# Two tiles begun on the un-normalised input behind three layer norms, and index items placed beside attention turns, in a two-block network on one core

## The chip, the cores and the metric

The kernel runs on one core of a Trainium2 chip. The metric is the device time in microseconds; the lower the better. The engines are TensorE (PE, matmuls; PEld its weight loads), VectorE (DVE), ScalarE (ACT), GpSimd (POOL) and SyncE (SP, which issues the weight transfers).

## The reference

Two blocks run one after the other on x of 512 positions by 1024 features, all in float32. The first block (RWKV, sparse attention, memory attention) isn't touched. The second has two layers; each is mixer, layer norm, SwiGLU, layer norm. The first mixer is a top-k attention, the second an HGRN2 recurrence:

```python
rel = relu(einsum('bqhd,bsd->bhqs', qib, k_idx))        # 8 index heads
score = einsum('bqh,bhqs->bqs', wb, rel)                # then the causal mask
_, sel = lax.top_k(score, topk)                         # softmax attention over sel
...
h = layer_norm(DEEPNORM_ALPHA * h + mix, ln_g[layer, 0], ln_b[layer, 0])
ffn = (silu(h @ w_gate[layer]) * (h @ w_up[layer])) @ w_down[layer]
h = layer_norm(DEEPNORM_ALPHA * h + ffn, ln_g[layer, 1], ln_b[layer, 1])
```

A layer norm is (x - mean)/sqrt(var + eps) * g + b over the 1024 features. So for a weight matrix W the product with a normalised position is r * (W'(g x)) + s * (W'g) + W'b, with r the inverse root and s = -mean * r of that position.

## The kernel before

x lies transposed, as 8 tiles (k) of 128 features by 512 positions. All dense weights come as a stream of 229 slabs of 128 by 1024 (one output tile of 128 features, 8 k). SP loads them into a ring of four (`load_slabs`, line 101); a slab's place in the ring is free when it is split. Each slab and each input is cut in a high part, which ACT casts to the fast matmul type (`cast_slab`, line 145), and a low part, which DVE takes as the difference (`split_slab`, line 150). `product` (lines 176 to 178) does a tile with three matmuls: high by high, high by low, low by high. A slab against the whole input is 24 matmuls of 128 by 512. Two slabs hold parts at a time (three in HGRN); `place_third` gives one slab further room.

The program is a list of stages. Between two stages all engines meet at a barrier. Within one, each engine runs its own hand-written list, tied by semaphores. The stages here are: `stage_dsa` (attention), `stage_project` "wo", `stage_ffn` 0, `stage_hgrn`, `stage_project` "ho", `stage_ffn` 1, `stage_store`.

A layer norm is cut over two stages. `Norm` ends the first. Per output tile DVE adds the residual (lines 1935, 2137) and sums x (1747), ACT squares (1730), POOL adds squares (1738). PE sums the accumulators and the last tile over the features by ones-columns (1758, 64 instructions in all), DVE and ACT make r and s (1795 to 1806), PE does four warm-up matmuls (184), then spreads r and s over 128 rows (1777). ACT and DVE cast and split the next three slabs. `Apply` opens the second stage: DVE multiplies by r and adds s (1831, 1834), ACT applies g and b twice, for the high part and for x (1845, 1847), POOL takes the low part (1853). PE does ten warm-ups and then `first_pair`, the first two slabs k by k as low parts come; then the other slabs.

In `stage_ffn` slabs alternate between gate and up. ACT takes Silu of the gate bank (2081) and casts the product (2084), DVE multiplies (2115) and takes its low part (2118); eleven turns of two hidden tiles. In `stage_hgrn` each of 8 heads has four slabs: forget gate (sigmoid), value, query (Silu), output gate (Silu), taken by ACT at line 2848 into SBUF; between them it does Ln (2878) and four Exps (2886 to 2896) for the decays. PE's `turned` transposes values and keys (2745, 2751) into banks 2 and 3; inner products begin at line 2765.

In `stage_dsa` 24 index items (3 query blocks of 128 positions by 8 heads; the first block needs none) go first: PE makes the scores against all keys so far (2589; 256, 384 or 512 columns), ACT takes Relu (2604), DVE adds them up with the head's weight (2619, 2622). Then follow 68 turns of `Attend`, one a unit (a head of a query block): PE scores (1204), DVE masks and takes the minimum (1257), ACT takes Exp (1235), three turns later PE transposes (1215) and a turn after sums (1226); a turn n has one `pick` for n up to 47 (2635, 2636), two DVE operations that find and strike the next eight largest scores. Sixteen picks make a block's mask, which the units 16 and more need. `fill` says how many warm-ups PE does ahead of a unit's transposes:

```python
fill = {n: 1 if n > 16 else 2 for n in range(4, len(units)) if begin.group_of(n + Attend.TURN, 0) is None} | {3: 10, 16: 6}
```

Of the kernel before, what the change touches and what calls it, by code (L numbers as in the profile page):

```python
# [6 lines left out]
F32 = mybir.dt.float32  # L7
# [60 lines left out]
class Ctx:  # L68
# [58 lines left out]
    def place_third(self, n, tile):  # L127

        at = self.bigr[:, tile:tile + 4, :].rearrange("p a b -> p (a b)")
        self.third = {n: at.rearrange("p (a k c) -> p a k c", a=2, k=KT)}  # L130
# [9 lines left out]
    def cast_slab(self, act, n, i=0):  # L140

        act.wait_ge(self.slab_ready[n % RING], 16 * (n // RING + 1) + i * 16)
        if n >= self.held and n not in self.third:
            act.wait_ge(self.slab_done, n - self.held + 1 + i * RING)
# [64 lines left out]
def first_pair(c, pe, slab, x):  # L209
# [3 lines left out]
    for k in range(KT):  # L213
        x.wait(pe, k)
        for u in range(2):
            mm = product(pe, c.bank[u][:, :], c.slab_parts(slab + u, k), x.tile(k), k == 0, k == KT - 1)
            if k == KT - 1:
                mm.then_inc(c.slab_done, 1)
# [104 lines left out]
def stage_in(c):  # L323
# [36 lines left out]
    with nc.Block() as block:  # L360
# [106 lines left out]
        def _(pe):  # L467
# [83 lines left out]
            first_pair(c, pe, 0, hp)  # L551
# [1160 lines left out]

class Norm:
# [4 lines left out]
    def __init__(self, c, tag, squares, at, kind, g, b=None, eps=1):  # L1718
        self.squares = squares
# [7 lines left out]

    def scalar_square(self, act, added, m):
        wait_tile(act, added, m)
        act.activation(self.squares[:, m, :], self.c.x[:, m, :], ACT.Square).then_inc(self.sq_out, 1)  # L1730

    def pool(self, pool):

        for m in range(1, KT - 1):
            pool.wait_ge(self.sq_out, m + 1)
            if m > 1:
                pool.wait_ge(self.sq_added, m - 1)
            pool.tensor_tensor(self.acc[:, 1, :], self.squares[:, 0, :] if m == 1 else self.acc[:, 1, :],
                               self.squares[:, m, :], ALU.add).then_inc(self.sq_added, 1)
# [10 lines left out]
    def tensor(self, pe, added):  # L1750

        c = self.c
        one = con(c, "ones")[:, 0:1]

        def sums(bank, x, first):
            for q in range(QT):
                for half in HALVES:
                    mm = pe.matmul(bank[half, q:q + 1], x[:, q * P:(q + 1) * P][:, half], one, start=first and q == 0,
                                   stop=not first, skip_group_check=True)
            return mm  # L1760

        wait_tile(pe, added, KT - 3)
        if self.kind == "ln":
            pe.wait_ge(self.x_added, KT - 2)
            sums(c.bank[0], self.acc[:, 0, :], True)
        pe.wait_ge(self.sq_added, KT - 2)
        sums(c.bank[1], self.acc[:, 1, :], True)
# [1493 lines left out]
```

## Time and profile before

| | us |
|---|---|
| median of three runs | 1902.44 (1901.03 to 1903.01) |
| the profiled execution | 1900.69 |
| its span | 1898.8 |
| PE busy | 1811.3 (95%) |
| DVE busy | 897.9 (47%) |
| ACT busy | 781.5 (41%) |
| POOL busy | 246.2 (13%) |

The span is what the trace covers; 1.9 us of the execution lie around it. Matmuls are pipelined: their rows overlap, and the distance between starts is the cost of one. The granted clock of PE is given as a share of 2.4 GHz, so 0.50 is the lower level, 1.2 GHz. Rows of a timeline give start, duration, engine, line, operation, result and operands, shape, count, and in brackets the idle time before it with what ended it. All times of rows count from the span's start.

### The profile page before, as it was taken

The page shows a single profiled execution, that of the slowest core. Times are in us where ns is not written, and L with a number is a line of the kernel's source. Part 1 is how long each engine was busy: PE and PEld are TensorE (multiplying, and loading weights), DVE is VectorE, ACT ScalarE, POOL GpSimd, SP SyncE. Part 2 cuts the span into 40 slices and gives each one's busy share as a digit, 9 for nine tenths or more (in the row PEclk, how much of TensorE's full clock was granted, in tenths as well). Part 3 has the DMA queues.
Part 4 walks back from the last instruction along what each step waited for, and adds up shares of the span by engine and source line. Part 5 has one row for each costly group of instructions (what it writes and reads, how often), then busy time and mean ns, then how long its engine had stood idle before and what let it go on. Part 6 is the DMA issues. An engine that isn't in the chain of part 4 may idle for free. (4 is left out here: it accounts for less than half of the span.)

```text
span 1898.8 us, 31549 instructions
## 1 busy us (share of the span) xinstructions
PE 1811.3 (95%) x12642; PEld 1419.9 (75%) x12642; DVE 897.9 (47%) x1644; ACT 781.5 (41%) x1341; POOL 246.2 (13%) x205
## 2 busy tenths in 40 slices
PE   6999999899899899999999999999998999999996
PEld 5776666576775666778888888788887778888885
DVE  2673554555557796343333323654554533333223
ACT  4543444455443445342323222765563333222222
POOL 3011232000125000120000000322320210000000
PEclk9999999899999899999999999999999999999998
DMA  5231101200121000213323233222221222332331
GB/s 185 89 92 66 35 25 36 84 23 12 45 74 45 1 1 1 75 64 95 99 99 91 97 100 98 66 87 69 77 67 31 92 75 91 99 99 94 95 100 45
DMA packets 38488, 134.00 MB, mean 71 GB/s; under 512 B 4896, under 2 KB 5344, under 8 KB 38112
## 3 DMA queue, kind: packets, MB, share of 16 engines
q1 hardware_dynamic: 37504, 130.07, 21.5%
q8 instruction: 87, 1.43, 0.3%
q10 hardware_dynamic: 864, 2.23, 0.3%
q14 instruction: 33, 0.27, 0.0%
HBM read 129.40 MB, written 2.10 MB: 69 GB/s over the span
## 5 line engine op out<-in xcount | busy, mean ns | idle before, releaser
L150 DVE TENSOR_TENSOR big_parts<-ring,big_parts 128x1024 fp32r<-128x1024 f32 x181 | 226.7, 1256 | 532.6 <-ACT big_parts L145 531.2
L176 PE MATMUL bank<-h_parts,big_parts 128*128 128x512 f32 (+1 forms) x1072 | 423.9, 395 | 8.3 <-DVE big_parts L150 4.9
L177 PE MATMUL bank<-y_parts,big_parts 128*128 128x512 f32 (+1 forms) x1072 | 417.2, 389 | 0.0
L178 PE MATMUL bank<-h_parts,big_parts 128*128 128x512 f32 (+1 forms) x1072 | 417.2, 389 | 0.0
L145 ACT ACTIVATE big_parts<-ring 128x1024 fp32r<-128x1024 f32 x181 | 191.3, 1060 | 382.9 <-PE bank L178 380.1
L176 PEld LDWEIGHTS bank<-h_parts,big_parts 128*128 128x128 f32 x1072 | 201.9, 188 | 59.0 <-POOL y_parts L1853 6.8
L178 PEld LDWEIGHTS bank<-h_parts,big_parts 128*128 128x128 f32 x1072 | 201.8, 188 | 42.0
L177 PEld LDWEIGHTS bank<-y_parts,big_parts 128*128 128x128 f32 x1072 | 202.0, 188 | 39.4
L176 PE MATMUL bank<-big_parts 128*128 128x512 f32 x352 | 136.9, 389 | 0.0
L177 PE MATMUL bank<-work_parts,big_parts 128*128 128x512 f32 x352 | 136.9, 389 | 0.0
L178 PE MATMUL bank<-big_parts 128*128 128x512 f32 x352 | 136.9, 389 | 0.0
L1235 ACT ACTIVATE work<-work 128x256 f32<-128x256 f32 (+4 forms) x128 | 67.1, 524 | 110.9 <-DVE work L1257 110.5
L184 PE MATMUL bank<-cst 128*128 128x256 f32 x356 | 101.1, 413 | 8.2 <-PEq L92 8.2
L176 PE MATMUL bank<-h_parts,work_parts 128*128 128x512 f32 x232 | 93.9, 405 | 1.2 <-PEq L92 0.8
L184 PEld LDWEIGHTS bank<-cst 128*128 128x128 f32 x356 | 70.8, 207 | 28.1 <-issue 15.5
L1257 DVE CUSTOM_DVE_ANT_0 work<-bank,big 128x256 f32<-128x256 f32 (+4 forms) x128 | 56.8, 444 | 73.2 <-PE bank L1204 63.7
L178 PE MATMUL bank<-h_parts,work_parts 128*128 128x512 f32 x232 | 90.5, 390 | 0.0
L177 PE MATMUL bank<-y_parts,work_parts 128*128 128x512 f32 x232 | 90.4, 390 | 0.0
L832 PE MATMUL bank<-x,ring 128*128 128x512 f32 x176 | 85.7, 610 | 0.2 <-ACT big L1031 0.2
L150 DVE TENSOR_TENSOR work_parts<-ring,work_parts 128x1024 fp32r<-128x1024 f32 x37 | 46.2, 1252 | 76.9 <-ACT work_parts L145 76.8
L177 PEld LDWEIGHTS bank<-work_parts,big_parts 128*128 128x128 f32 x352 | 66.1, 188 | 13.8
L176 PEld LDWEIGHTS bank<-big_parts 128*128 128x128 f32 x352 | 66.1, 188 | 13.7
(399 smaller groups left out, 2696.1 us busy)
## 6 DMA issues: line engine op xcount, KB each, us to landing
ring<-in_wstream SPq DMA_DIRECT2D x229, 512.0 KB, 3.6
x<-in_xt SPq DMA_DIRECT2D x8, 512.0 KB, 6.7
out_t<-x SPq DMA_DIRECT2D x8, 256.0 KB, 2.0
work<-in_memt ACTq DMA_DIRECT2D x1, 1024.0 KB, 14.2
y<-in_cw SPq DMA_DIRECT2D x1, 1024.0 KB, 5.0
cst<-in_cst ACTq DMA_DIRECT2D x1, 768.0 KB, 7.9
cos<-in_reset SPq DMA_DIRECT2D x2, 256.0 KB, 6.8
big<-work SPq DMA_DIRECT2D x4, 128.0 KB, 4.5
```

Of the source, the lines that this page charges most:

```text
L145: act.activation(self.place(n)[:, 0, :, :], self.ring[:, n % RING, :, :], ACT.Copy).then_inc(self.slab_cast, 1)
L150: dve.tensor_tensor(self.place(n)[:, 1, :, :], self.ring[:, n % RING, :, :], self.place(n)[:, 0, :, :].bitcast(F32), ALU.subtract).then_in ...
L176: pe.matmul(out, w[0], x[0], start=start, stop=False, skip_group_check=True)
L177: pe.matmul(out, w[0], x[1], start=False, stop=False, skip_group_check=True)
L178: return pe.matmul(out, w[1], x[0], start=False, stop=stop, skip_group_check=True)
L184: pe.matmul(bank[:, 0:2 * P], con(c, "ident"), c.cst[:, 0:2, :], start=True, stop=True)
L832: mm = pe.matmul(c.bank[DENSE_BANK][:, :], c.raw_slab(n, k), c.x[:, k, :], start=k == 0, stop=k == KT - 1)
L1235: act.activation(e, e, ACT.Exp, bias=self.low[:, n:n + 1], scale=-1.0, accum_out=self.den[:, n:n + 1])\
L1257: dve.tensor_tensor_reduce(self.weights(n), self.c.bank[self.SCORES[n % 3]][:, 0:u.keys], u.mask, -self.scale, 3e38, ALU.add, ALU.min, sel ...
```

## The change

Behind the norms of "wo", `stage_ffn` 0 and "ho" the first two slabs of the next stage are multiplied with g x, not with the normalised input. `Raw` makes the parts of g x per tile (ACT casts with g as scale, DVE takes the low part) in the stage before, and PE multiplies the raw slabs in the ring with the columns g and b (`columns`). The ones-column sums of the accumulators go ahead of the stage's last product (`early`), k = 0 and 1 of the two slabs stand where the warm-ups were, k = 2 to 7 open the next stage; there the second two slabs run k by k with the normalised input into banks 2 and 3. ACT copies the two finished banks, DVE applies r and s to them (`open_tile`), and W'b comes as a bias. Four slabs are cast and split by the stage's end, not three. In the feed-forward the fifth slab waits for the first product tile. In HGRN the fifth waits for the first taken tile, the first transposes for all four, and the lower-bound arithmetic `decays` comes behind the opened tiles.

In the attention 8 items stay ahead, with one warm-up between each; 16 go beside turns 0 to 11 (two beside each of the first four). For turns under 16 the pick comes last in the turn, and the fills of 10 and 6 are gone.

```diff
+class Raw:
+    BEGUN = 2
+    def scalar(self, act, k):
+        act.activation(self.hi[:, k, :], self.c.x[:, k, :], ACT.Copy, scale=vec(self.c, self.g[0], self.g[1] + k)).then_inc(self.cast, 1)
+    def vector(self, dve, k):
+        dve.wait_ge(self.cast, k + 1)
+        dve.scalar_tensor_tensor(self.lo[:, k, :], self.c.x[:, k, :], vec(self.c, self.g[0], self.g[1] + k),
+                                 self.hi[:, k, :].bitcast(F32), ALU.mult, ALU.subtract).then_inc(self.split, 1)
+    def columns(self, pe):
+        c = self.c
+        for u in range(2):
+            c.raw_wait(pe, self.slab + u)
+            for k in range(KT):
+                g, b = VECS[self.g[0]] + self.g[1] + k, VECS[self.b[0]] + self.b[1] + k
+                mm = pe.matmul(c.bank[2][:, 2 * u:2 * u + 2], c.raw_slab(self.slab + u, k), c.vecs[:, g:b + 1:b - g],
+                               start=u == 0 and k == 0, stop=k == KT - 1, skip_group_check=True)
...
 class Norm:
     def tensor(self, pe, added):
+        if self.raw:
+            self.raw.begin(pe, 0)
+        else:
+            self.early(pe, added)
         if self.kind == "ln":
             pe.wait_ge(added, KT)
-            sums(c.bank[0], c.x[:, KT - 1, :], False).then_inc(self.sums, 1)
+            self.column_sums(pe, self.sum_banks[0], c.x[:, KT - 1, :], False).then_inc(self.sums, 1)
         pe.wait_ge(self.sq_out, KT)
-        sums(c.bank[1], self.squares[:, KT - 1, :], False).then_inc(self.sums, 1)
-        warm(c, pe, c.bank[4], 4)
+        self.column_sums(pe, self.sum_banks[1], self.square(KT - 1), False).then_inc(self.sums, 1)
+        if self.raw:
+            for k in range(1, Raw.BEGUN):
+                self.raw.begin(pe, k)
+        else:
+            warm(c, pe, c.bank[4], 4)
...
     def vector(self, dve, ahead=None):
-        if ahead:
+        if self.raw:
+            self.raw.vector(dve, KT - 1)
+            self.raw.columns_out(dve)
+            for n in range(2, 4):
+                c.split_slab(dve, ahead + n)
+        elif ahead:
...
 class Apply:
+    def open_tile(self, dve, u):
+        c, n = self.c, self.n
+        dve.wait_ge(self.opened_raw, u + 1)
+        dve.tensor_tensor(self.opened[u], self.opened[u], n.spread_banks[0][:, :], ALU.mult).then_inc(self.opened_half, 1)
+        dve.wait_ge(self.opened_half, u + 1)
+        dve.scalar_tensor_tensor(self.opened[u], n.spread_banks[1][:, :], self.raw.columns_at[:, 2 * u:2 * u + 1], self.opened[u],
+                                 ALU.mult, ALU.add).then_inc(self.opened_out, 1)
...
 stage_ffn, tensor:
-            warm(c, pe, c.bank[4], 10)
-            first_pair(c, pe, gu, xp)
-            xp.wait_banks(pe)
-            for u in range(2, 4):
+            xp.raw_products(pe)
+            stream_pair(c, pe, gu + 2, xp, c.bank[2:4])
+            for u in range(4, 8):
+                pe.wait_ge(prod_out, 1 if u < 6 else 2)
                 gate_up(u, 0)
 stage_ffn, scalar:
             xp.scalar(act)
-            turn(0, True)
+            c.slab_done_wait(act, gu + 1)
+            c.cast_slab(act, gu + 4)
+            xp.copy_opened(act)
+            c.cast_slab(act, gu + 5)
+            xp.opened_wait(act, 0)
+            act.activation(silu[:, 0, :], xp.opened[0], ACT.Silu, bias=xp.opened_bias(0)).then_inc(silu_out, 1)
+            high(0, 0)
...
 stage_ffn, vector:
             xp.vector(dve)
-            turn(0, True)
+            c.split_slab(dve, gu + 4)
+            for u in range(2):
+                xp.open_tile(dve, u)
+            c.split_slab(dve, gu + 5)
+            dve.wait_ge(silu_out, 1)
+            xp.opened_wait(dve, 1)
+            dve.scalar_tensor_tensor(prod[:, 0, :], xp.opened[1], xp.opened_bias(1), silu[:, 0, :], ALU.add, ALU.mult).then_inc(prod_out, 1)
...
 stage_hgrn, tensor:
-                    pe.wait_ge(tile_out, u - 1)
+                    if u >= 4:
+                        pe.wait_ge(tile_out, u - 3 if u < 6 else u - 1)
...
-                pe.wait_ge(tile_out, 4 * h + 2)
+                pe.wait_ge(tile_out, 4 * h + 2 if h else 4)
...
-            warm(c, pe, c.bank[4], 10)
-            first_pair(c, pe, n0, xp)
-            xp.wait_banks(pe)
+            xp.raw_products(pe)
+            stream_pair(c, pe, n0 + 2, xp, c.bank[2:4])
 stage_hgrn, scalar and vector:
             xp.scalar(act)
+            xp.copy_opened(act)
+            c.cast_slab(act, n0 + 4)
...
             xp.vector(dve)
+            for u in range(2):
+                xp.open_tile(dve, u)
+            c.split_slab(dve, n0 + 4)
             decays()
...
 stage_dsa:
-    fill = {n: 1 if n > 16 else 2 for n in range(4, len(units)) if begin.group_of(n + Attend.TURN, 0) is None} | {3: 10, 16: 6}
+    fill = {n: 1 if n > 16 else 2 for n in range(4, len(units)) if begin.group_of(n + Attend.TURN, 0) is None}
+    twice, beside_end = 4, 12
+    beside = lambda n: range(IH + 2 * n, IH + 2 * n + 2) if n < twice else range(IH + twice + n, IH + twice + n + 1) if n < beside_end else ()
...
+            for n in range(IH):
+                item(n, n - 3)
+                warm(c, pe, c.bank[4], 1)
+            pe.wait_ge(relu_out, IH)
             for n in at.turns():
+                for x in beside(n):
+                    item(x, x - 1 if x >= IH + 2 else 0)
```

## Rows read from the trace of the kernel before

**Rows 1.** The page: busy time of each engine, and one group of weight loads.

```profile
PE 1811.3 (95%) x12642; PEld 1419.9 (75%) x12642; DVE 897.9 (47%) x1644; ACT 781.5 (41%) x1341; POOL 246.2 (13%) x205
...
L178 PEld LDWEIGHTS bank<-h_parts,big_parts 128*128 128x128 f32 x1072 | 201.8, 188 | 42.0
```

**Rows 2.** Windows: busy us (x instructions) of PE, PEld, DVE, ACT, POOL; clock, DMA, GB/s.

```profile
1000.00:1100.00 100.00, 100.00 (x443) 82.84 (x442) 32.38 (x34) 29.31 (x35) 0.00 (x0) 1.00 0.32 99
```

**Rows 3.** Timeline of PE, attention output to first feed-forward: start us, us, instruction xcount.

```profile
818.49 1.10 PE L1758 MATMUL bank<-cst,work 128*64 128x1 f32 x32
819.45 0.61 PE L1758 MATMUL bank<-cst,x 128*64 128x1 f32 x16
...
823.43 2.58 PE L1777 MATMUL bank<-cst,work 128*128 128x128 f32 x16
...
831.88 0.47 PE L176 MATMUL bank<-h_parts,big_parts 128*128 128x512 f32 x1 [0.52 <-POOL y_parts L1853]
```

**Rows 4.** Timeline of DVE at the same place (idle before it and its releaser in brackets).

```profile
818.60 0.69 DVE L1935 SCALAR_TENSOR_TENSOR x<-x,bank 128x512 f32<-128x512 f32 x1 [4.02 <-PE bank L178]
...
822.23 3.50 DVE L150 TENSOR_TENSOR big_parts<-ring,big_parts 128x1024 fp32r<-128x1024 f32 x3 [0.57 <-ACT big_parts L145]
826.80 1.29 DVE L1831 TENSOR_TENSOR x<-x,bank 128x512 f32<-128x512 f32 x2 [1.07 <-PEq L92]
```

**Rows 5.** Timeline of POOL there, first and last of eight.

```profile
830.46 1.27 POOL L1853 TENSOR_TENSOR y_parts<-x,h_parts 128x512 fp32r<-128x512 f32 x1 [14.58 <-ACT x L1847]
...
841.37 1.29 POOL L1853 TENSOR_TENSOR y_parts<-x,h_parts 128x512 fp32r<-128x512 f32 x1 [0.27 <-ACT x L1847]
```

**Rows 6.** Timeline of ACT in the first feed-forward.

```profile
840.48 0.81 ACT L1847 ACTIVATE x<-x,vecs 128x512 f32<-128x512 f32 x1
...
866.18 1.06 ACT L145 ACTIVATE big_parts<-ring 128x1024 fp32r<-128x1024 f32 x1 [3.75 <-PE bank L178]
```

**Rows 7.** Timeline of PE from the first feed-forward to HGRN.

```profile
1192.47 1.10 PE L1758 MATMUL bank<-cst,work 128*64 128x1 f32 x32
...
1242.33 0.89 PE L2765 MATMUL bank<-work 128*64 128x32 f32 x24
```

**Rows 8.** Timelines of DVE (first row) and ACT in HGRN.

```profile
1200.55 0.69 DVE L1831 TENSOR_TENSOR x<-x,bank 128x512 f32<-128x512 f32 x1 [0.85 <-PEq L92]
...
1217.88 0.60 ACT L2848 ACTIVATE big<-bank 128x512 f32<-128x512 f32 x1
...
1219.44 1.28 ACT L2878 ACT_TABLE_LOAD   x1
...
1231.04 0.59 ACT L2848 ACTIVATE big<-bank 128x512 f32<-128x512 f32 x1
```

**Rows 9.** Timelines of PE and ACT, HGRN output to second feed-forward.

```profile
1503.30 0.87 PE L1758 MATMUL bank<-cst,work 128*64 128x1 f32 x24
...
1539.85 1.06 ACT L145 ACTIVATE big_parts<-ring 128x1024 fp32r<-128x1024 f32 x1 [3.87 <-PE bank L178]
```

**Rows 10.** Timeline of DVE in the top-k attention.

```profile
619.71 4.95 DVE L2622 SCALAR_TENSOR_TENSOR work<-work 128x384 f32<-128x384 f32 x7 [0.21 <-ACT work L2604]
...
625.40 5.90 DVE L2622 SCALAR_TENSOR_TENSOR work<-work 128x512 f32<-128x512 f32 x7 [0.35 <-ACT work L2604]
...
647.59 0.29 DVE L1257 CUSTOM_DVE_ANT_0 work<-bank,big 128x128 f32<-128x128 f32 x1 [5.54 <-issue]
...
671.14 0.69 DVE L2569 TENSOR_TENSOR big<-bank,work 128x512 f32<-128x512 f32 x1 [2.51 <-PE bank L1226]
```

**Rows 11.** Timeline of PE there, fill of two warm-ups, one turn apart.

```profile
647.29 1.03 PE L184 MATMUL bank<-cst 128*128 128x256 f32 x4
...
648.95 1.03 PE L184 MATMUL bank<-cst 128*128 128x256 f32 x4
```

**Rows 12.** Windows, turns 0 to 15 of the attention (columns as in rows 2).

```profile
632.50:661.80 29.30, 25.51 (x144) 19.35 (x145) 19.81 (x86) 11.05 (x46) 0.00 (x0) 0.83 0.00 1
```

**Rows 13.** Windows, PE alone: busy (x), granted clock, DMA share, GB/s.

```profile
614.00:616.00 2.00, 2.00 (x6) 0.50 0.00 0
```

More of the change, by code:

```diff
@@ L215, in first_pair @@
         for u in range(2):
-            mm = product(pe, c.bank[u][:, :], c.slab_parts(slab + u, k), x.tile(k), k == 0, k == KT - 1)
+            mm = product(pe, banks[u][:, :], c.slab_parts(slab + u, k), x.tile(k), k == 0, k == KT - 1)
             if k == KT - 1:
@@ L1748, in vector_add, with column_sums, early @@
                               ALU.add).then_inc(self.x_added, 1)
[L1750 to L1760, printed above, removed]
+    def column_sums(self, pe, bank, x, first):
+        for q in range(QT):
+            for half in HALVES:
+                mm = pe.matmul(bank[half, q:q + 1], x[:, q * P:(q + 1) * P][:, half], con(self.c, "ones")[:, 0:1],
+                               start=first and q == 0, stop=not first, skip_group_check=True)
+        return mm
+    def early(self, pe, added):
         wait_tile(pe, added, KT - 3)
@@ L1882, in stage_project, with here @@
     added = c.sem(f"{tag}_added")
-    norm = Norm(c, tag, c.big, 10, *norm)
-    c.place_parts(*parts)
+    ahead = slab + KT
+    raw = Raw(c, tag, ahead, *norm[1:], wkr(c, T, KT, T), wkr(c, 12 * T, KT, T))
+    norm = Norm(c, tag, c.big, 10, *norm, raw=raw)
     c.norm = norm
+    def here():
+        c.place_parts(*parts)
+        c.place_apart(ffn_apart(ahead))
+    here()
     yp = parts_of(c, f"{tag}_y", c.y if src is None else src)
@@ L1906, in _ @@
                         yp.wait(pe, k)
+                    if m == KT - 1 and k == KT - 1:
+                        norm.early(pe, added)
                     mm = product(pe, c.bank[m][:, :], c.slab_parts(slab + m, k), yp.tile(k), k == 0, k == KT - 1)
@@ L2009, in stage_ffn, with here, onward @@
         ("added", "silu_out", "prod_out", "hidden_cast", "hidden_out"))
-    xp = Apply(c, f"{tag}x")
-    norm = Norm(c, tag, c.h, 27, "ln", ("ln_g", (2 * layer + 1) * KT), ("ln_b2", (2 * layer + 1) * KT))
+    xp = Apply(c, f"{tag}x", opened=[wk(c, (29 + u) * T, T) for u in range(2)])
+    g, b = ("ln_g", (2 * layer + 1) * KT), ("ln_b2", (2 * layer + 1) * KT)
+    raw = None if layer else Raw(c, tag, dn + FT, g, b, c.yr, c.hr)
+    norm = Norm(c, tag, c.h if layer else c.big[:, 22:24, :], 27, "ln", g, b, raw=raw)
     silu, prod = wk(c, T, 2, T), wk(c, 3 * T, 2, T)
     hid, hid_lo = c.bigr, wkr(c, 5 * T, FT, T)
-    c.place_parts(*ffn_parts(c))
     c.norm = norm
+    def here():
+        c.place_parts(*ffn_parts(c))
+        c.place_apart(ffn_apart(gu))
+    def onward():
+        c.place_apart({} if layer else hgrn_apart(dn + FT))
+    here()
     down_made = c.sem(f"{tag}_down_made")
@@ L2063, in _ @@
                     pe.wait_ge(hidden_out, j + 1)
+                if raw and m == KT - 1 and j == FT - 2:
+                    norm.early(pe, added)
                 mm = product(pe, down_bank(m), c.slab_parts(dn + n // KT, n % KT), (hid[:, j, :], hid_lo[:, j, :]),
@@ L2599, in _, with item @@
         def _(act):
-            for n, (q, h) in enumerate(items):
+            def item(n):
+                q, _ = items[n]
                 act.wait_ge(made, n + 1)
@@ L2603, in _ @@
                     act.wait_ge(taken, n - 2)
-                act.activation(relu[:, n % 3, 0:(q + 1) * P], c.bank[n % 4][:, 0:(q + 1) * P], ACT.Relu).then_inc(relu_out, 1)
+                act.activation(relu[:, n % 3, 0:(q + 1) * P], item_bank(n)[:, 0:(q + 1) * P], ACT.Relu).then_inc(relu_out, 1)
+            for n in range(IH):
+                item(n)
             for n in at.turns():
+                for x in beside(n):
+                    item(x)
                 at.scalar_turn(act, n)
@@ L2612, in _, with item @@
             ch = Chain(dve, chain)
-            for n, (q, h) in enumerate(items):
+            def item(n):
+                q, h = items[n]
                 w = (q + 1) * P
@@ L2880, in _ @@
                         act.wait_ge(vt_made, s - 1)
-                    taken(4 * s + 1, vv[s % 2], ACT.Copy)
+                    taken(4 * s + 1, vv[s % 2], ACT.Copy if s else ACT.Identity)
                     act.wait_ge(diff_out, 4 * s + 1)
```

251 lines of the change are left out of this document (177 added, 74 removed).

## The prediction

> **What bounds the kernel now.** I read the page first: TensorE (PE) is busy for 95% of the span, VectorE (DVE) for 47%, ScalarE (ACT) for 41% [rows 1]. The stages of 100 us show where PE is simply full: in the first feed-forward it has 443 matmuls in 100 us, 0.226 us each at the full 2.4 GHz clock [rows 2]. A weight slab is 24 such matmuls, 5.44 us, one k of a pair of slabs 1.36 us. So only the places where PE does nothing useful can give time back. The timeline finds them: four layer-norm junctions (three lie before a projection, the fourth before the store and is not touched), and the opening of the top-k attention.
>
> At a junction the last product is over when the ones-column sums begin. After the attention output that is 818.49, and the first product of the next stage is at 831.88 [rows 3]. The reader should see the order in between: last tile added 818.60, statistics ready 821.66 (the splits' start less their idle 0.57), three slab splits until 825.73, next stage's DVE at 826.80 [rows 4]. Then POOL's low parts come from 830.46 to 841.37, 1.56 us apart [rows 5], slower than PE's 1.36 us. The warm-up matmuls make PE look busy here; they are no work.
>
> **The change at the feed-forward junctions.** Times count from S0, the first sum of the old trace (818.49, 1192.47, 1503.30 [rows 3, 7, 9]).
>
> Moved: the 32 ones-column instructions of the accumulators, 0.96 us by start to start (the row's 32 begin at 818.49, the x sums of the row after them at 819.45, [rows 3]). They stand before the last product now: still PE's time, but off the statistics' chain. Their inputs were ready long before.
>
> Added: 16 full-precision matmuls with 128-column weights from the ring, 32 instructions, that make W'g and W'b. The trace has no such shape. The nearest row is the 64-column sums, 0.96/32 = 0.030 us each [rows 3]: 1.0 us as the low end. The high end is the 16 spreading instructions that stream 128 columns, 2.58 us, 0.16 each [rows 3]: 5.2 us. The low row is nearer, in its short moving side; the weights are twice as wide: I take a little over twice it, 2.2 us. The Trainium skill ("TensorE: Matmul & The Clock Gate", Back-to-back issue gap) gives about 81 ns for each weight-load-and-matmul pair at 128 columns. By that it would be 2.6 us, as an estimate, and the total gain 1.2 us smaller; no row here shows the pair.
>
> So the last product ends at S = S0 + 3.15. Raw k=0 runs (1.36 us) while DVE adds the last tile (0.69), then the sums, then raw k=1. Statistics are ready near S+3.5, PE spreads until S+5.8. DVE does one low part (0.7), a small copy and two splits (1.17 each) in place of three: done at S+6.85, against S0+7.24 before. The stage ends 1.07 us later (826.80 less 825.73 [rows 4]); so B, the next stage's start, is about S0+11.1, not S0+8.3. What the copy waits for and the last low part's input (ACT's copy, ended S+2.2) are early.
>
> In that stage PE runs raw k=2 to 7 at once: 36 matmuls, B+8.3. The second pair then needs normalised tiles. The last low part lands at B+15.9 (841.37+1.29 less 826.80 [rows 4, 5]), before PE asks for it at B+17.8, so the pair runs unbroken to B+19.2. This is the cover that the change buys.
>
> But the fifth slab waits for the first product tile. ACT finishes the normalising at B+14.5 [rows 6], then casts gu+4 (1.06), copies two banks (0.5 apart), casts gu+5. DVE behind it splits gu+4 (1.2), opens two tiles (two operations of about 0.7 each, 2.8), splits gu+5 (1.2) and only then multiplies the first tile (0.75). That is B+21.5. **PE stands about 2.3 us** there, and nothing else is queued that it could do. Six slabs end at B+32.4 = S0+43.5. Before, the sixth was done when ACT began a cast on it, 866.18 = S0+47.6 [rows 6]. Gain 4.1 us.
>
> Behind the last hidden-layer norm of the HGRN output the same, with a start of 0.78 us: S0+43.2, against the fourth slab done at 1539.85 and two more, 1550.7 = S0+47.4 [rows 9]. Gain 4.2 us. The extra ACT copy and DVE subtraction per tile (0.65 and 0.75 us) in the stages before lie in slab periods of 5.44 us; DVE's chain there, cast 1.06, split 1.23, low part 0.75, two adds 1.4, is 4.5 us: hidden, with 1 us left.
>
> **The change at the HGRN junction.** Same head, with 0.85 us between stages: B = S0+10.85, raw products to B+8.3, pair to B+19.2. The saved PE time meets a chain on ACT. ACT ends normalising at B+14.5, two copies, one cast (B+16.7). The lower-bound arithmetic on DVE now stands behind the opened tiles and a split, so it starts at B+18.8, its exponential comes at B+19.4 and the sigmoid, with a table load of 1.28 us [rows 8], at B+20.95. Before it was at 1217.88, B+17.3 [rows 8]. From sigmoid to the fourth taken tile took 13.75 us (1217.88 to 1231.63 [rows 8]); two slab casts leave this chain, which saves 2.4: the fourth tile is out at B+32.3.
>
> PE waits for the first (dense 4, about 19.2 to 21.6), ends it at B+27.0, and then its first transposes wait for **all four tiles**, as they write banks 2 and 3 that held the last two: idle from 27.0 to 32.3. One more slab and it is B+38.7 = S0+49.55. Before, the sixth slab was over at 1242.33 = S0+49.86 [rows 7]. Gain 0.3 us: the 10.9 us freed go into two stalls of 7.7 us, and the rest into the later B. After that both versions are full.
>
> **The top-k attention.** Before: 24 items are bound by DVE, seven of 384 columns in 4.95 us and seven of 512 in 5.90 [rows 10], over at 631.3. Then turns 0 to 15 to 661.8, in which DVE is busy 19.8 of 29.3 us [rows 12]: 9.1 idle, 5.54 of it in one piece behind ten warm-ups [rows 10]. PE starts this stage at half clock (0.50, that is 1.2 GHz [rows 13]).
>
> After: 16 items (8 at 0.70, 8 at 0.84, 12.3 us) go beside turns 0 to 11. Same DVE work, so the most that can be won is the idle time, 9.1 us. Against it: a warm-up between the first eight items doubles PE's part while the clock is low; they end near 622.1, by my count, where they ended at 619.1. Turns 0 to 3 then take 2.6 us of DVE (1.2 + 2 items), turns 4 to 6 2.03. From turn 7 PE has a two-warm fill (4 instructions, about 0.9 us; PE's turn was 1.66, 647.29 to 648.95 [rows 11]) and now an item of 512 columns, 5.90/7 = 0.84 at PE's pace [rows 10]: 2.5 us a turn, so PE paces turns 7 to 10. Turn 11 waits for a group's sum (3.6), turn 12 adds two causal masks (1.8). Sum: turn 16 starts near 659.8, not 661.8. Then the fill of six at unit 16 shrinks to two, 4 x 0.43 = 1.7 us of the 2.51 that DVE waited at 671.14 [rows 10]. Gain 3.7 us; ends -3 (the later items and nothing back) and 9.1 + 2.5 = 11.6. DVE is the pacer up to 720, so it carries on.
>
> **Sum.** 4.1 + 4.2 + 0.3 + 3.7 = 12.3 us off the profiled execution's 1900.69: 1888.4. The median of the runs is 1.75 above that execution, so 1890.1; I say 1890.
>
> **Rivals.**
> 1. The openings don't stall: the first product or the fourth tile comes before PE asks for it. Then the feed-forwards gain 4.1 + 2.3 and 4.2 + 2.3, HGRN 0.3 + 7.7, in all 20.9, with the attention 24.6: time 1878. For it: DVE and ACT queues may run nearer than I add them up. Against: the ACT rows are back to back there [rows 8].
> 2. The clock. The attention's turns 0 to 6 leave PE partly idle; in the old turns the mean granted clock was 0.83 [rows 12]. If it drops to the lower level there, PE's turns double: 3.2 for 2.6 four times, 3.3 for 2.03 three times, 6 us lost: time 1896. The Trainium skill (same page, What's actually happening) says that an idle PE goes to 1.2 GHz; the trace agrees, with 0.50 behind the change of stages at 612 [rows 13].
> 3. **Slower.** The column matmuls don't overlap: fresh weights for each, so load and matmul follow one another. A load lasts 0.188 us in the mean [rows 1], and the last of the 32 sums ran 1.10 less 31 x 0.030 = 0.17: 0.36 an instruction, 11.5 us for 32, at three junctions 27.9 more than I count: 1918. It decides above (2.2 + 12.3/3) = 6.3 us a junction. Against: 32 loads and matmuls of the sums fit in 0.96 us [rows 3].
> 4. The change does not do what it says: opened tiles are late by more than 2 us at each feed-forward (ACT's chain pushed by POOL or table loads), and the attention wins nothing: gain 3 us or less, 1899.
>
> **How the numbers follow.** About 0.2% (3.8 us) is what a measurement of this kernel can tell from no change. My forecast 0.55; rival 1 0.15; rival 2 0.13; rival 3 0.06; rival 4 0.11. The forecast's own ends: columns at 1.0 give 3.6 us more, an attention gain of 8 gives 4.3, together 1882; an attention at -3 costs 6.7, 1897; columns at 5.2 cost 9.0, 1899. To hold 8 in 10 the range reaches towards rival 1 and rival 2: 1880 to 1898. Rival 3 and part of 1 and 4 stay out. Faster takes the first three cases and a little of 4, less the slow end of 2: 0.84; same 0.09; slower 0.07.
>
> **What would show it.** At each junction, raw products with no idle before them and the second pair directly behind; a PE wait of 2 to 2.5 us for the first product tile in both feed-forwards; in HGRN two waits, some 2.4 and 5.3 us, the second before the transposes; 32 column instructions in about 2.2 us; turn 16 of the attention near 660 and a DVE idle share there under a fifth. Wrong would be: column rows above 6 us, PE half-clocked in turns 0 to 6, or the second pair waiting for low parts.

## The result, and the profile after

The changed kernel takes **1905.5 us** in the median of 20 runs (1900.5 to 1909.1), the kernel before 1901.8 in 20 runs beside it (1900.3 to 1905.4): the medians are 3.7 us apart, and the ratio of the runs is 1.0015, 95% interval 1.0009 to 1.0022. So it is slower, by a little. Forecast were 1890 and a range of 1880 to 1898; direction and range are wrong. The profiled execution of the changed kernel took 1904.01 us, its span is 1902.2, 3.4 more than before.

The busy times of the page say as little as they did in [rows 1]:

```profile
PE 1809.8 (95%) x12642; PEld 1422.8 (75%) x12642; DVE 919.0 (48%) x1683; ACT 797.2 (42%) x1371; POOL 245.2 (13%) x205
```

So I read the timeline of PE at the places of the forecast. Columns: start us, us, instruction, count, in brackets the idle time before it and what ended it. First the junction behind the attention output, against [rows 3], then the HGRN junction, the first slab behind the bank wait in each feed-forward (852.23, 1541.33), and HGRN's two waits:

```profile
814.65 1.10 PE L1810 MATMUL bank<-cst,work 128*64 128x1 f32 x32
815.68 5.28 PE L1738 MATMUL bank<-vecs,ring 128*128 128x2 f32 x32
820.82 0.77 PE L176 MATMUL bank<-h_parts,work_parts 128*128 128x512 f32 x1
821.39 0.63 PE L177 MATMUL bank<-y_parts,work_parts 128*128 128x512 f32 x1
821.82 0.63 PE L178 MATMUL bank<-h_parts,work_parts 128*128 128x512 f32 x1
...
824.72 0.63 PE L1810 MATMUL bank<-cst,x 128*64 128x1 f32 x16
...
827.25 1.95 PE L1845 MATMUL bank<-cst,work 128*128 128x128 f32 x16
830.66 0.47 PE L176 MATMUL bank<-work_parts,big_parts 128*128 128x512 f32 x1 [1.46 <-PEq L92]
...
852.23 0.50 PE L176 MATMUL bank<-h_parts,big_parts 128*128 128x512 f32 x1 [2.25 <-DVE work L2299]
...
1189.40 3.73 PE L1738 MATMUL bank<-vecs,ring 128*128 128x2 f32 x32
1193.00 0.74 PE L176 MATMUL bank<-big_parts 128*128 128x512 f32 x1
...
1203.54 0.47 PE L176 MATMUL bank<-y_parts,big_parts 128*128 128x512 f32 x1 [1.55 <-PEq L92]
...
1225.44 0.47 PE L176 MATMUL bank<-h_parts,big_parts 128*128 128x512 f32 x1 [2.58 <-ACT big L3068]
...
1236.06 1.11 PE L2965 MATMUL bank<-cst,big 128*128 128x128 f32 x4 [4.89 <-ACT big L3071]
...
1508.07 0.77 PE L176 MATMUL bank<-h_parts,big_parts 128*128 128x512 f32 x1
...
1541.33 0.80 PE L176 MATMUL bank<-h_parts,big_parts 128*128 128x512 f32 x1 [2.28 <-DVE work L2299]
```

There are two things to see. The 32 column instructions (L1738) last 5.14 us from their start to the next product; 3.60 at the second junction, and 4.07 (1504.00 to 1508.07) at the third. And behind them the products follow one another every 0.43 us (821.39 to 821.82), where full speed is 0.226 [rows 2]. The windows of PE alone (busy us, count, granted clock, DMA share, GB/s) say why:

```profile
815.70:820.80 5.10, 5.10 (x34) 0.68 0.01 3
820.80:824.50 3.70, 3.70 (x10) 0.51 0.00 0
824.50:828.00 3.50, 3.50 (x47) 1.00 0.00 0
1193.00:1195.00 2.00, 2.00 (x7) 0.51 0.00 0
1508.00:1512.00 4.00, 4.00 (x10) 0.50 0.00 0
1512.00:1516.00 4.00, 4.00 (x38) 0.50 0.00 0
```

**The granted clock is at its lower level, 1.2 GHz, behind every column block**, although PE is busy in every one of these windows: it stays there 3.7, about 3.5 and 9.4 us. In the first and the third block it had fallen already before their end (0.68 in the first); with that part the low stretches are 6.8, 3.4 and 10.2 us long. Inside the second block the clock is full, so 3.60 us is the block's own length, and the rest of 5.14 and 4.07 is the clock's.

Stretch by stretch, in the profiled executions (S0 of the new kernel is its first sum plus 0.68, the issue time of the three matmuls that now stand behind it):

- Start of the program to the start of the top-k attention's stage: 612.48 before, 616.01 after, 3.5 later. The kernels are the same there; see the last section.
- That start to S0 at the attention output: 206.0 to 199.3, gain 6.7.
- On to S0 behind the first feed-forward: 374.0 to 373.7, gain 0.3 (forecast 4.1).
- On to S0 at the HGRN output: 310.8 to 314.6, loss 3.8 (forecast a gain of 0.3).
- On to the start of the store's stage: 382.0 to 385.1, loss 3.1 (forecast a gain of 4.2).

From S0 to B, the start of the next stage, it is 15.3, 14.5 and 16.1 us (830.66 less 815.33, and so on), against 11.1, 10.85 and 10.8 forecast: 13.2 us in all. That alone is more than the gain that the forecast adds up to.

In the attention, the timeline of DVE:

```profile
646.21 0.29 DVE L1257 CUSTOM_DVE_ANT_0 work<-bank,big 128x128 f32<-128x128 f32 x1 [0.50 <-DVE work L2841]
...
652.47 0.69 DVE L2755 TENSOR_TENSOR big<-bank,work 128x512 f32<-128x512 f32 x1 [0.81 <-PE bank L1226]
...
660.85 0.29 DVE L2843 TENSOR_SCALAR big<-work 128x256 f32<-128x256 f32 x1
...
668.00 0.69 DVE L2755 TENSOR_TENSOR big<-bank,work 128x512 f32<-128x512 f32 x1 [0.24 <-PE bank L1226]
```

The one piece of 5.54 us in [rows 10] is gone, and the 2.51 at the fill of six are 0.24. The mask that ends block 1 (L2843) comes 44.8 us after the stage's start; before, 48.1 (660.61). The same window as [rows 12] of all engines now shows DVE busy for 25.3 us instead of 19.8, and the clock at 1.00 instead of 0.83:

```profile
632.50:661.80 29.30, 26.39 (x150) 17.41 (x150) 25.31 (x87) 14.28 (x50) 0.00 (x0) 1.00 0.00 1
```

### The profile page after: what moved, and what is told of

It is laid out like the page before. It is cut to its first block and busy times, and to the rows that moved or that the text cites. A ratio compares the mean times of both kernels' runs of the same rounds, so it can differ in the third digit from the quotient of the medians.

```text
span 1902.2 us, 31615 instructions
## 1 busy us (share of the span) xinstructions
PE 1809.8 (95%) x12642; PEld 1422.8 (75%) x12642; DVE 919.0 (48%) x1683; ACT 797.2 (42%) x1371; POOL 245.2 (13%) x205
## 5 line engine op out<-in xcount | busy, mean ns | idle before, releaser
L176 PE MATMUL bank<-h_parts,big_parts 128*128 128x512 f32 (+1 forms) x1024 | 404.3, 395 | 12.8 <-DVE big_parts L150 4.9
L177 PE MATMUL bank<-y_parts,big_parts 128*128 128x512 f32 (+1 forms) x1024 | 399.3, 390 | 0.0
L178 PE MATMUL bank<-h_parts,big_parts 128*128 128x512 f32 (+1 forms) x1024 | 399.2, 390 | 0.0
L176 PEld LDWEIGHTS bank<-h_parts,big_parts 128*128 128x128 f32 x1024 | 193.7, 189 | 55.2 <-DVE work L2299 5.4
L178 PEld LDWEIGHTS bank<-h_parts,big_parts 128*128 128x128 f32 x1024 | 193.5, 189 | 40.5
L177 PEld LDWEIGHTS bank<-y_parts,big_parts 128*128 128x128 f32 x1024 | 193.8, 189 | 38.0
L177 PE MATMUL bank<-work_parts,big_parts 128*128 128x512 f32 x384 | 151.3, 394 | 0.0
L1794 POOL TENSOR_TENSOR work<-big 128x512 f32<-128x512 f32 x4 | 5.2, 1296 | 623.7 <-ACT big L1784 623.7
L177 PEld LDWEIGHTS bank<-work_parts,big_parts 128*128 128x128 f32 x384 | 73.2, 191 | 15.3
L184 PE MATMUL bank<-cst 128*128 128x256 f32 x260 | 79.2, 420 | 3.0 <-PEq L92 3.0
## 6 DMA issues: line engine op xcount, KB each, us to landing
work<-in_memt ACTq DMA_DIRECT2D x1, 1024.0 KB, 14.3
```

The lines of the kernel that those rows point to most:

```text
L176: pe.matmul(out, w[0], x[0], start=start, stop=False, skip_group_check=True)
L177: pe.matmul(out, w[0], x[1], start=False, stop=False, skip_group_check=True)
L178: return pe.matmul(out, w[1], x[0], start=False, stop=stop, skip_group_check=True)
L184: pe.matmul(bank[:, 0:2 * P], con(c, "ident"), c.cst[:, 0:2, :], start=True, stop=True)
L1794: pool.tensor_tensor(self.acc[:, 1, :], self.square(0) if m == 1 else self.acc[:, 1, :], self.square(m), ALU.add).then_inc(self.sq_added, 1)
```

## The experiments

Each time is a median, in brackets the kernel before in the same session.

**Which part lost: three kernels.** e1_no_columns leaves W'g and W'b out of the computation; the corrections are then made from what is in the bank. All waits and copies stay.

```diff
-        self.column_sums(pe, self.sum_banks[1], self.acc[:, 1, :], True)
+        mm = self.column_sums(pe, self.sum_banks[1], self.acc[:, 1, :], True)
         if self.raw:
-            self.raw.columns(pe)
+            mm.then_inc(self.raw.cols_made, 1)
```

> The changed kernel without the 32 column instructions at each of the three junctions (W'g and W'b are left out, so the opened tiles are wrong; all waits, copies and the opened tiles' arithmetic stay). Theory 1, the columns and the low clock behind them are what the junctions lose: 5.1 + 3.6 + 4.1 us of column rows go, and with the clock kept some 2 us more at each, so 15 to 21 us below the changed kernel and 12 to 18 below the one before. Theory 2, the waits for the opened tiles are the loss and the columns only fill a time in which PE would have waited: within 4 us of the changed kernel.

e2_attention_only is the kernel before with the new `stage_dsa`, e3_junctions_only the changed kernel with the old one.

> The kernel before with only the attention's items moved beside the turns. In the profiles the stretch from the attention's start to the end of the output projection is 206.0 us before and 198.6 after. Theory 1, the attention gains and the junctions lose: 5 to 8 us below the kernel before. Theory 2, the 198.6 is mostly a luckier clock in that one execution: 0 to 3 us below.

> The changed kernel with the old attention: only the three junctions are changed. Theory 1: slower than before by 7 to 11 us (what the changed kernel loses plus the attention's gain). Theory 2, the attention gains nothing: slower by 2 to 5 us.

Measured: e1 1884.6 (1902.2), ratio 0.991 (0.989 to 0.992); e2 1896.1, 0.997 (0.996 to 0.998); e3 1911.7, 1.005 (1.004 to 1.006). All three lie where the first theory of each put them. The attention wins 6.1 us and the junctions lose 9.5; together 3.4 slower, as the whole change (3.7). Without the column instructions the changed kernel would be 20.9 us faster, 7.0 for each junction. In e1 the first sums are at 813.59 and the next stage begins at 823.03: 8.8 us from S0 to B; the other two junctions have 9.3 and 8.6. The forecast's values without the columns are 11.1 - 2.2 = 8.9, 8.65 and 8.6. So the rest of the head was added up right to 0.7 us, and the columns, with the clock behind them, are the miss there.

**Length, or clock?** e7_columns_twice makes every column product twice.

```diff
-        for u in range(2):
+        for n in range(4):
+            u = n % 2
             c.raw_wait(pe, self.slab + u)
```

> The changed kernel with every column matmul done twice (64 instructions a junction; the second pass overwrites the first). If one costs 0.11 to 0.16 us of PE, it is 3.6 to 5.1 us more a junction, and the clock, already low behind the first, falls no further: 12 to 17 us above the changed kernel, 1917 to 1922. If PE had waited there anyway: within 3 us.

Measured: 1923.4 (1902.0), ratio 1.011 (1.010 to 1.013): 17.9 above the changed kernel, just outside the 12 to 17, 6.0 a junction. Timeline of PE, first junction:

```profile
814.39 11.70 PE L1739 MATMUL bank<-vecs,ring 128*128 128x2 f32 x64
825.95 0.77 PE L176 MATMUL bank<-h_parts,work_parts 128*128 128x512 f32 x1
```

Its window shows the clock at 0.50 throughout the second half of the block, with 29 instructions in 5.9 us, 0.20 us each. The block at full clock is 0.11 each (3.60/32 at the HGRN junction). A second block costs about its own length at the lower clock (32 x 0.20 = 6.4, measured 6.0). There is one fall of the clock, not two, but it lasts longer: 13.7 us at 0.50 at each of the three junctions (816.7 to 830.4 at the first), where the changed kernel has 6.8, 3.4 and 10.2.

e10_filler_for_columns is e1 (again W'g and W'b are left out) with ten warm-up matmuls of 256 streamed columns where the columns stood.

```diff
         if self.raw:
             mm.then_inc(self.raw.cols_made, 1)
+            warm(self.c, pe, self.c.bank[2], 10)
```

> The kernel without columns (W'g and W'b left out), with ten warm-up matmuls of 256 columns, 4.35 us at full clock, in the place of each block of column instructions. Theory 1, the block costs its own time and besides lets the clock fall: a block of the same length with the array streaming costs its length alone, 13.0 us above the 1884.6 of the kernel without columns: 1896 to 1899, 6 to 9 below the changed kernel. Theory 2, any such block costs as much as the columns do, since what is late behind it decides: 1903 to 1907.

Measured: 1894.4 (1902.7), ratio 0.996 (0.994 to 0.997). Timeline of PE:

```profile
814.67 4.58 PE L184 MATMUL bank<-cst 128*128 128x256 f32 x20
818.90 0.58 PE L176 MATMUL bank<-h_parts,work_parts 128*128 128x512 f32 x1
819.32 0.39 PE L177 MATMUL bank<-y_parts,work_parts 128*128 128x512 f32 x1
819.55 0.40 PE L178 MATMUL bank<-h_parts,work_parts 128*128 128x512 f32 x1
```

Its windows of PE show the full clock in the filler and behind it; so it is at the other two junctions:

```profile
814.67:818.90 4.23, 4.23 (x25) 1.00 0.01 4
818.90:824.00 5.10, 5.10 (x51) 1.00 0.00 0
```

The filler takes 4.23 us a junction, 12.7 for three, and the three column blocks 12.8. Yet this kernel is 11.1 us faster than the changed one, more than the 6 to 9 of the first theory: as much PE time, and products at full pitch behind it (819.32 to 819.55). That separates two costs: **by the medians a block's length costs 9.8 us** (e10 less e1) **and the lower clock 11.1** (the changed kernel less e10).

The sizes of the two are known less well than the medians suggest. From the first sum to the next stage the three heads take 28.7 us in e1's profile, 41.5 in e10's and 48.0 in the changed kernel's: 12.8 for the length and 6.5 for the clock. The granted clock over a whole run shows why the medians divide it otherwise. It is 0.979 in the median of the changed kernel's 20 runs (0.976 to 0.981), 0.986 in e10's five (0.984 to 0.987) and 0.983 to 0.986 in e1's four. As an estimate from these shares, the changed kernel gives up some 13 us more to the clock than e10, and e1 some 5 us more than e10, which hides a part of the filler's length. So the clock costs 6.5 to 11 us here, and it shows in every run: the clocks of the changed kernel and of e10 don't overlap. What in the block lowers the clock is not separated: the filler streams 256 columns for 2, but it also has 20 instructions, each with its weights, for 32.

**Columns in small pieces.** e4_columns_between makes the columns of one k, four instructions, ahead of each of the last eight products, so that no long run of them arises.

```diff
+                    if m == KT - 1:
+                        raw.columns(pe, k, added, 3)
                     mm = product(pe, c.bank[m][:, :], c.slab_parts(slab + m, k), yp.tile(k), k == 0, k == KT - 1)
...
+                if raw and m == KT - 1 and j >= FT - KT:
+                    raw.columns(pe, j - FT + KT, added, KT - 1)
```

> The changed kernel with the same column instructions, two matmuls ahead of each of the last eight products of the stage and no longer in one block. Theory 1a, a lone column instruction is slow because its 128-column full-precision weight load has no stream to hide under, and the low clock comes from the block: here the loads hide under 512-column streams and the clock stays, 10 to 18 us below the changed kernel. Theory 1b, the load costs PE the same 0.13 us wherever it stands: the 4 us stay at each junction and only the clock is kept, 3 to 8 us below the changed kernel. Theory 2: within 3 us.

Measured: 1893.9 (1902.2), ratio 0.996 (0.994 to 0.997): 11.6 faster than the changed kernel, 9.3 slower than e1. The size is in the range of theory 1a, but the rows show the mechanism of 1b, the price unchanged and the clock kept; 1b had put too little on the clock. Timeline of PE:

```profile
808.64 0.50 PE L1740 MATMUL bank<-vecs,ring 128*128 128x2 f32 x4
809.01 0.48 PE L176 MATMUL bank<-h_parts,work_parts 128*128 128x512 f32 x1
...
809.79 0.50 PE L1740 MATMUL bank<-vecs,ring 128*128 128x2 f32 x4
```

One k takes 1.15 us (808.64 to 809.79) instead of 0.68, so four column instructions cost 0.46, **0.115 each, even with streams on both sides**; 3.7 a junction. The clock is 1.00 here. Behind the first feed-forward it still dropped, for 3.3 us at 1188.70 (0.51), without one long block: spreading them made the fall rarer, not impossible. Counted over all profiles, the clock fell in or behind the block at all 9 junctions of the changed kernel, e3 and e7. With the columns in pieces (e4, and e5, e6 and e9 below) it fell at 1 of 12, and without columns (e1, e10) at none of 6.

**The waits.** e5_bank_wait is e4 with the fifth and sixth slab of the feed-forwards waiting for what they need, the copy of their bank, and not for the first product tile.

```diff
             for u in range(4, 8):
-                pe.wait_ge(prod_out, 1 if u < 6 else 2)
+                if u < 6:
+                    pe.wait_ge(xp.opened_raw, u - 3)
+                else:
+                    pe.wait_ge(prod_out, 2)
                 gate_up(u, 0)
```

> The kernel with the columns between the products (its profile shows the two feed-forwards waiting 2.3 us for the first product tile), and the fifth and sixth slab now wait only for the copy of the bank that they write. Theory 1, that wait is a real loss on PE's path: 4.5 us less from the two waits, up to 7 if the low clock behind them goes too, so about 1888 to 1889. Theory 2, the wait is given back because the next slab's split or the first hidden tile is late anyway: within 1.5 us of 1893.9.

Measured: 1888.5 (1902.0), ratio 0.993 (0.992 to 0.994): 5.4 faster than e4. The two waits are 2.3 us each, 4.6; the remaining 0.8 may be the clock, but is too small for these medians to show. In e4 and in the changed kernel the products behind the second wait start at half speed (1541.33, then 0.43 apart up to 1544.5); in e5 neither the waits nor the slow products are there.

e6_hgrn_order is e5 with the same loosening in HGRN, PE's second dense slab ahead of the first transposes, one cast and one split moved forward, and the lower-bound arithmetic ahead of the opened tiles.

```diff
-                    if u >= 4:
-                        pe.wait_ge(tile_out, u - 3 if u < 6 else u - 1)
+                    if u in (4, 5):
+                        pe.wait_ge(xp.opened_raw, u - 3)
+                    elif u >= 6:
+                        pe.wait_ge(tile_out, u - 1)
...
+                if s == 1:
+                    dense(5)
                 if s >= 1:
                     turned(s - 1)
-                if 1 <= s < HG:
+                if 2 <= s < HG:
```

> The same, and in HGRN: the fifth and sixth slab wait for the bank copies alone, the sixth slab runs before the first transposes, its cast and split come earlier, and the lower-bound arithmetic comes before the opened tiles. Theory 1: of the 2.6 and 4.9 us that PE waits there, and some 2 us of low clock behind them, 5 to 8 us come back: about 1881 to 1884. Theory 2, the chain of takings on ACT sets the time there and PE only waits elsewhere (for the inner products): under 2 us less than the kernel with the bank wait.

Measured: 1888.2 (1902.0), ratio 0.993 (0.992 to 0.995): nothing against e5, as theory 2 has it. The timeline of PE shows the waits moved, not gone:

```profile
1227.55 0.66 PE L2975 MATMUL bank<-cst,big 128*128 128x128 f32 x4 [2.58 <-ACT big L3083]
1228.05 0.60 PE L2981 MATMUL bank<-cst,work 128*128 128x128 f32 x4
1232.40 3.63 PE L2995 MATMUL bank<-work 128*64 128x32 f32 x64 [3.76 <-DVE work L3230]
...
1239.15 0.63 PE L177 MATMUL bank<-y_parts,big_parts 128*128 128x512 f32 x1
```

6.3 us of waiting where 7.5 was, and the clock at its lower level behind them. The second wait ends with DVE's L3230 (four small multiplies), and DVE's timeline shows it queued behind a weight split that waits for its cast:

```profile
1228.48 2.26 DVE L150 TENSOR_TENSOR big_parts<-ring,big_parts 128x1024 fp32r<-128x1024 f32 x1 [5.33 <-ACT big_parts L145]
1230.66 1.69 DVE L3230 TENSOR_TENSOR work<-work,big 128x128 f32<-128x128 f32 x4
```

e9_inner_keys_first therefore puts that work ahead of the split, in the first turn.

```diff
-                split(4 * s + 6)
+                if s:
+                    split(4 * s + 6)
                 inner_keys(s)
+                if not s:
+                    split(6)
```

> The kernel with the HGRN order, and for the first head DVE multiplies the inner keys before it splits the seventh slab (which waits for ACT's cast behind the fourth taking). In the profile of the HGRN order PE waited 3.8 us for these keys, with 5 us of low clock behind. Theory 1, the wait only moved to the split's place in DVE's queue: 3 to 6 us less than the HGRN order, about 1883 to 1885. Theory 2, the head is bound by ACT's chain (value and key copies come behind the next sigmoid): under 1.5 us.

Measured: 1886.8 (1902.7), ratio 0.992 (0.991 to 0.994): 1.4 less than e6, by size theory 2. The wait of 3.76 is gone all the same:

```profile
1228.06 0.66 PE L2975 MATMUL bank<-cst,big 128*128 128x128 f32 x4 [2.54 <-ACT big L3083]
...
1232.93 2.63 PE L3008 MATMUL bank<-work 64*128 64x128 f32 x14 [0.54 <-ACT work L3113]
1235.49 0.79 PE L176 MATMUL bank<-h_parts,big_parts 128*128 128x512 f32 x1
1236.09 0.63 PE L177 MATMUL bank<-y_parts,big_parts 128*128 128x512 f32 x1
```

HGRN's stage is 3.5 us shorter than in e6 in the profiles (260.9 for 264.4), but the medians differ by 1.4, and the intervals of the two overlap; whether the gain is real is open. Products still start at half speed.

e8_columns_split is e6 with half of the columns behind the spreading matmuls, where PE waits for the change of stages in any case.

```diff
             mm.then_inc(self.spread, 1)
+        if self.raw:
+            for k in range(4, KT):
+                self.raw.columns(pe, k, added, 0)
```

> As the kernel with the HGRN order, and only four of the eight k's columns stand between products; the other four come behind the spreading matmuls, where the profiles show PE idle 1.5 us before the stage ends. Theory 1, they fill idle time: 1.5 us less at each junction, 3 to 5 us in all. Theory 2, they pull the stage's end out by their whole length, or the clock drops behind them: no gain, or up to 5 us slower.

Measured: 1886.6 (1902.0; its runs reach from 1886.2 to 1893.7), ratio 0.992 (0.991 to 0.994): 1.7 below e6, which the intervals don't tell apart. Timeline and windows of PE:

```profile
827.03 1.84 PE L1740 MATMUL bank<-vecs,ring 128*128 128x2 f32 x16
```

```profile
829.90:833.00 3.10, 3.10 (x9) 0.66 0.60 170
1199.70:1203.00 3.30, 3.25 (x8) 0.51 0.68 200
1515.20:1519.00 3.80, 3.75 (x17) 1.00 0.67 199
```

The sixteen instructions are partly covered: the idle time before the next stage shrinks from 1.45 to 0.99 us at the first junction, and the way from the first sum to that stage grows by 0.8, 0.3 and 0.8 us for 1.84 that are taken out ahead of it. In two of three junctions the next stage then begins at a lower clock. But this is the slowest of the five executions (1893.7), so whether the clock takes the gain back in the others isn't shown.

e5, e6, e8 and e9 beat both kernels; their medians lie within 2 us of one another, and 13.5 to 15.9 us below the kernel before.

## Why the prediction was wrong

**The step that failed is the cost of the column matmuls**, "I take a little over twice it, 2.2 us". By e1 they cost 7.0 us a junction, and that has two parts, the price of an instruction and a clock that I left out.

**The price:** I chose between 1.0 and 5.2 by the row with the short moving side; it is 3.60 at full clock and up to 5.14, 0.11 to 0.16 us each. The spreading row (0.16), my high end, shares with them the 128-column full-precision weights, and it was the nearer one. It was itself taken partly at the lower clock (0.74 in its window). The same 16 instructions at the third junction of the kernel before ran at full clock:

```profile
1507.20 1.95 PE L1777 MATMUL bank<-cst,work 128*128 128x128 f32 x16
```

That is 0.12 each, for 128 streamed columns, and the column instructions with 2 took 0.11. By this row I would have said 3.9 us a junction, close to the 3.60 of the second. The Trainium skill's figure in the same step ("TensorE: Matmul & The Clock Gate", Back-to-back issue gap) gave 2.6 us. Its figure is for 128 streamed columns; with 2 the trace's 0.111 an instruction at full clock is still above its 81 ns, so that would also have come out too low. At full clock my value is worth (3.60 - 2.2) x 3 = 4.2 us of the miss.

**The missing term, and the larger part: the clock in and behind the block.** None of my terms changed PE's speed at the junctions. Without this term even my high end, 5.2 us a block, gives 1899, not 1905.5. I had put the lower level on places where PE is partly idle (rival 2, in the attention). It was the other way round: in those turns the clock was 1.00, and it was 0.50 behind blocks in which PE counts as busy all the time. The Trainium skill's section of rival 2 (same page, What's actually happening) speaks of an idle PE; the windows above show a fall that the busy share does not announce.

The sum: e1 says that the blocks cost 20.9 us with all that they bring, where I had 6.6. Of the 14.3 us between the two 4.2 are the price, and the other 10.1 I put down to the clock, about half of the 20.4 us that it was low. Less the 2.4 that the attention gave more than forecast, that is 11.9 of the 15.5 us between forecast and median. The other 3.6 don't come with the columns, as e1 shows: it should have been at 1881.0 by my sum and is at 1884.6. In its profile they lie in HGRN (a gain of 0.1 for 2.5) and in the last stretch (4.4 for 6.4), where the products behind the waits run at half speed (see **The waits**).

**The head otherwise:** right. e1 has 8.8 us from S0 to B against 8.9. Raw products ran without idle, the second pair of tiles directly behind.

**The waits:** right in place and size. First product tile 2.25 and 2.28 (forecast about 2.3), HGRN 2.58 and 4.89 (2.4 and 5.3), their releasers the ones named. Rival 1 (no stalls) falls with that. What I left out is that slow products can follow them: behind the second of the feed-forward waits and behind HGRN's second, up to 1.8 us each (eight products at 0.43 instead of 0.23 behind 1541.33). Where they fall changes between executions: e3 has them behind the first feed-forward's wait as well, and is 3.2 us longer in that feed-forward (376.1 from stage to stage, for 372.9), part of it a longer column block (4.57 for 3.60).

```profile
856.12 0.80 PE L176 MATMUL bank<-h_parts,big_parts 128*128 128x512 f32 x1 [2.27 <-DVE work L2299]
856.71 0.63 PE L177 MATMUL bank<-y_parts,big_parts 128*128 128x512 f32 x1
857.14 0.63 PE L178 MATMUL bank<-h_parts,big_parts 128*128 128x512 f32 x1
```

**The gains by stretch** then follow: 4.1 less 4.2 of a later B leaves nothing in the first feed-forward (measured 0.3). HGRN's 0.3 less 3.6 is -3.3 (measured -3.8). What the clock takes behind its second wait, up to 1.8, would make it -5.1; a wait 0.4 shorter than forecast gives a part of that back, and about 0.9 stays unexplained. The last one's 4.2 less 5.3 and less about 1.8 is -2.9 (measured -3.1).

**The attention:** right mechanism, too small: 3.7 forecast, 6.1 measured by e2. At the mask of block 1 3.3 us are won (forecast 2.0), at full clock; a turn with two warm-ups and a 512-column item is 2.52 us (646.21 to 648.73), as forecast, so the difference lies in the turns before it: turns 0 to 3 took 9.9 us for 10.4, 4 to 6 5.3 for 6.1, and turns 7 and 8 4.2 for 5.0, with a start 1.2 later than counted. The fill of six gave 2.3 (1.7). Of the 6.7 of the profile's stretch about 1 us is left; it comes later in the stage and was not looked into. A part of the gain is clock: the old attention has 10.2 us at 0.50 in these turns (633.6 to 643.8, and the same in e3), and its ten warm-ups, half of them in that stretch, take 5.95 us; the new one has no such stretch.

**The rivals:** rival 3 had the right sign and the right place, a column block dearer than I take it. Its price, 0.36 an instruction without any overlap, is not what happened: 0.11 at full clock. Its threshold (6.3 us a junction) was reached by the sum of block and clock, 7.0 us by e1, not by the block alone. Rival 2 did not happen (clock 1.00 in the turns), nor rival 4: the opened tiles were in time, the waits no more than 0.2 us longer than forecast, and the attention gained.

## What to carry to other kernels

Price full-precision matmuls by their weights, not by what they stream: with 128-column weights an instruction cost 0.115 us here even between long streams, and 0.11 to 0.12 whether it streamed 2 columns or 128, so 32 of them are 3.7 us of an engine that is full. Before such a block is put into a busy TensorE, ask also what the granted clock will be behind it, and look at the clock of small windows: a page with 95% busy shows nothing of it. Where the work can't go, put it in small pieces between streams, and let a slab wait for its bank and not for the later result that happens to free it.

## What the runs showed of the hardware that I had not expected

- The clock falls in or behind a block of two-column matmuls in which PE is never idle: 32 instructions in 3.6 to 5.1 us, then 1.2 GHz for 3.5 to 9.4 us. A block of the same length that streams 256 columns an instruction leaves it at 1.00. Behind sixteen such instructions (1.84 us) and a change of stages it was at 0.66 and 0.51 in e8's profile at two junctions, and at 1.00 at the third. Why the second junction's block ran at full clock inside, and the third's low stretch is the longest, is open; in e3 all three low stretches are 6.8 us.
- Times of code that no kernel here changed vary: the top-k attention's stage starts between 612.5 and 618.9 us in the twelve profiled executions. The before's is the lowest. So the 3.4 us between the two profiled spans lie in unchanged code (3.5), and the changed stretches come out even (a gain of 0.1), while the medians of e2 and e3 sum to a loss of 3.4. The profiles show where time goes; how much it is in all only the medians tell. The granted clock goes along with the difference: up to that start PE is at the lower level for 17.1 us in the kernel before, for 30.7 in the changed one, for 20.5 to 27.3 in the eight profiles that start there between 613.5 and 615.0, and for 34.1 in the two latest (617.2 and 618.9). Half of the 13.6 us between the first two would be 6.8, more than the 3.5 seen, so not all of it lies where PE sets the time. Why the clock differs in the same code was not tried.
